# Queries and keys as seven block products per pair of panels, with the sums of the input formed in the gating stage

## Chip, cores and metric

One core of a Trainium2 chip runs the kernel. The metric is device time in microseconds (us) of one execution; less is better.

## What is computed

One step of a hybrid decoder layer for 512 prompt tokens and 64 sample tokens, 576 in all, with a model width of 1024. Cut to what matters here:

```
h = rmsnorm(x); z = h @ w_in                  # w_in: 1024 wide in, split into q, k, v, u, s, m and gates
q, k, v = zq, zk, zv                          # 1024 columns each: differential attention
o_sg = gelu(zu) * mix(rmsnorm(gelu(zs)))      # chunked spatial gating
merged = g0 * (o_da @ wb0) + g1 * (o_sg @ wb1) + g2 * (o_mx @ wb2)
x = x + merged @ w_out
a, b = split(rmsnorm(x) @ w_up); x = x + (silu(a) * b) @ w_down
```

The keys, the values and the normalised rows of s are outputs as well.

## The kernel before

Activations are kept transposed, 8 tiles of 128 features by 576 tokens. Every product is taken in three matmuls, of numbers split into a high and a low part in the fp32r type: hi times hi, lo times hi, hi times lo. Weights come in panels of 128 output columns (512 KB each) from one stream in HBM, `w_stream`, in the order of `STAGES`: mk and mv (memory keys and values), s, q, k, v, u, da_gate, and so on to w_out, the pairs of up, and down. A **plain panel** (`panel`, L1895) is 8 tiles x 3 terms x 2 halves of 288 tokens, 48 matmuls into a bank pair `acc[u]`. For each panel SP loads `w_raw[u]`, ScalarE copies it to `w_hi[u]` (`split_hi`, L696), VectorE forms `w_lo[u]` (`split_lo`, L1183), and ScalarE evacuates the result.

Each engine's program is written out by hand, and semaphores tie them together; nothing is scheduled by a planner. In the stage s the result goes through a gelu and is turned by TensorE in the next panel's shadow (`turning`, `turn_tile`), and VectorE copies it to `s_nat` (`nat_copy`). While q runs, ScalarE squares `s_nat`, GpSimd forms the factors (`g_rs`) and VectorE normalises (`nat_norm`, L1324). Each panel of k is followed by one mixing product of the gating (`mix`, L2053), and the panels of v are turned like those of s.

Only the stage up is done in **pairs**: 22 units of two panels, one of a, one of b. A unit splits its 2 x 2 blocks (weight halves by token halves) into seven products of 4 tiles x 3 terms, 84 matmuls of 128x288 (`product`, L2349). VectorE forms four weight sums per unit (`pair_sums`) and seven low parts (`lo_of`, L1585), ScalarE seven high parts (`hi_of`, L1061) and three copies of partial results (`product_copy`), and VectorE adds the partial results up (`up_unit`). The sums of the input (`xs_raw`, `xs_hi`, `xs_lo`) are formed tile by tile behind w_out's residual additions (L1595 to L1620). Products 0 to 3 of a unit have their split weights in the panel buffers `w_hi` and `w_lo`, products 4 to 6 in buffers of their own, `w_hi_b` and `w_lo_b`. The first unit's four weight sums are GpSimd's (L1873), and they begin once w_out's seventh panel is done. The norm's statistics of the new x (`norm_stats(2)`) run after product 1 of the first unit, and their broadcast after product 3.

Of the kernel before, what the change touches and what calls it, by code (L numbers as in the profile page):

```python
# [28 lines left out]
P = 128  # L29
# [28 lines left out]
STAGES = (("mk", 8), ("mv", 8), ("s", 8), ("q", 8), ("k", 8), ("v", 8), ("u", 8), ("da_gate", 8),  # L58
# [8 lines left out]
PAIRS = (("up", FT),)  # L67
# [5 lines left out]
STREAM_AT = {"up": FIRST["down"], "down": FIRST["down"] + 2 * FT}  # L73
# [4 lines left out]
BANK_OF = ("x", "z", "x", "z", "x", "w", "x")  # L78
BANK_START = (True, True, False, False, False, True, False)
# [24 lines left out]
def decoder_layer(nc, xT, memT, w_stream, page_table, cache_k, cache_v, mem_k, mem_v, consts,  # L104
# [3 lines left out]
    with ctx:  # L108
# [66 lines left out]
        nat_square, = at(merged_at, ("nat_square", [P, QT + 1, D]))  # L175
        sg = Region(x_at)
        norm_b = sg.take("norm_b", [P, D])
        sgb_b = sg.take("sgb_b", [P, GROUPS, P])
        sg_w = sg.take("sg_w", [P, GROUPS, P])
        sg_ws = Region(diag_at).take("sg_ws", [NS, GROUPS, NS])  # L180
# [82 lines left out]
        def pair_bank(j, s):  # L263

            return {"x": acc[0][:, s, 0:HT], "z": acc[1][:, 0, 0:HT], "w": acc[1][:, 1, 0:HT]}[BANK_OF[j]]

        def pair_raw(s, n, k):

            return (w_raw, w_raw_b)[s][:, n, k * KW:(k + 1) * KW]

        def pair_hi(j):
            return w_hi[:, j // 2, j % 2 * KW:(j % 2 + 1) * KW] if j < 4 else w_hi_b[:, j - 4, :]

        def pair_lo(j):
            return w_lo[:, j // 2, j % 2 * KW:(j % 2 + 1) * KW] if j < 4 else w_lo_b[:, j - 4, :]

        def pair_s(j, i=1):
            if isinstance(i, int) and i == 0:
                return w_sum[:, 1, :] if j == 1 else w_sum_b[:, {2: 1, 3: 2, 4: 0}[j], :]
            return w_sum[:, j, :] if j < 4 else w_sum_b[:, j - 4, :]  # L280
# [228 lines left out]
        def _(sp):  # L509
            def load_w(p, u, off=0):  # L510
# [4 lines left out]
            def stream(start, end, off=0):  # L515
# [4 lines left out]
            def load_pair(i, s, at):  # L520
# [3 lines left out]
                for n in range(2):  # L524
                    sp.dma_start((w_raw, w_raw_b)[s][:, n, :],
# [26 lines left out]
            for c in range(2):  # L552
                sp.dma_start(m_x[:, 4 * c:4 * c + 4, :], memT[4 * c * P:(4 * c + 4) * P, :]
                             .rearrange("(k p) n -> p k n", p=P)).then_inc(mem_loaded[c], 16)
                load_w(c, c)
# [5 lines left out]
            stream(2, FIRST["s"] + 4)  # L561
# [3 lines left out]
            stream(FIRST["s"] + 4, FIRST["s"] + 6)  # L565
            sp.wait_ge(line_stored, 16)
            for c in range(2):
# [5 lines left out]
            stream(FIRST["s"] + 6, FIRST["q"] + 2)  # L573
# [1939 lines left out]
```

## Time and profile before

| | us |
|---|---|
| median of 3 runs | 1344.37 (1343.51 to 1346.86) |
| the profiled execution | 1343.05 |
| its span | 1341.3 |
| TensorE busy in it | 1315.5 (98%) |
| VectorE, ScalarE, GpSimd busy | 667.9, 524.5, 89.9 |

The mean granted clock of TensorE is 0.992 of full speed. How to read it: TensorE is busy nearly throughout, so its timeline gives the stages' borders, and its few idle stretches lie at such borders. What TensorE waits for there is read from the timelines of VectorE, ScalarE and GpSimd in the same microseconds. Busy times of those three are averages over stages with different limits.

### The profile page before, as it was taken

The numbers are of one execution on the slowest core, as the hardware profiler recorded it, in microseconds if no ns is written. First come the engines' busy times: TensorE is split into PE (matmuls) and PEld (weight loads), VectorE is DVE, ScalarE is ACT, GpSimd is POOL, SyncE is SP. The second block draws the span as 40 slices with busy tenths as digits, with TensorE's granted clock in tenths as the row PEclk, the third lists the DMA queues.
The fourth block names the chain that finished last, engine by engine and source line by source line (L and its number), as shares of the span: only waits on it lengthen the run. The fifth ranks groups of instructions, "written<-read, shape, count | busy, mean of one in ns | idle before, by whom it ended". The sixth has DMA issues, their size and how long they took to land.

```text
span 1341.3 us, 25811 instructions
## 1 busy us (share of the span) xinstructions
PE 1315.5 (98%) x10082; PEld 1245.4 (93%) x10082; DVE 667.9 (50%) x1167; ACT 524.5 (39%) x1010; POOL 89.9 (7%) x129
## 2 busy tenths in 40 slices
PE   8899999999999999999999999998999999999997
PEld 8889999999888888888988889998999999999997
DVE  6643232223566532222344323567888888863333
ACT  5432321223477632222422343245555555552220
POOL 3620000000001010000000000001000000000001
PEclk9999999999999999999999999998999999999998
DMA  6544222524222197776589111432222222222221
GB/s 240 165 154 163 81 87 76 197 102 150 71 75 71 53 304 226 260 247 207 195 321 342 61 48 48 148 106 72 93 94 94 94 94 94 94 79 90 84 94 71
DMA packets 82087, 179.10 MB, mean 134 GB/s; under 512 B 5869, under 2 KB 40941, under 8 KB 80982
## 3 DMA queue, kind: packets, MB, share of 16 engines
q1 hardware_dynamic: 77750, 158.31, 34.7%
q10 hardware_dynamic: 2496, 12.58, 2.6%
q0 software_dynamic: 1760, 7.08, 1.5%
q8 instruction: 57, 0.93, 0.3%
q14 instruction: 24, 0.20, 0.0%
HBM read 166.13 MB, written 14.18 MB: 134 GB/s over the span
## 4 chain that ended last, share of the span: by engine, by line
PE 62%; issue 31%; DVE 2%; POOL 2%; ACT 1%; DMA 1%; POOLq 0%; SPq 0%; DVEq 0%; ACTq 0%
PE acc L1895 49%; PE ps L2107 2%; PE ps L2088 2%; PE ps L2164 1%; PE ps L2141 1%; PE ps L2272 1%; POOL ssum L1765 1%; PE ps L2288 1%; PE ps L2098 1%; PE ps L2239 1%; PE ps L1922 1%; PE ps L2053 1%; PE ps L2221 1%; DVE w_lo L1183 0%; DMA m_x<-memT 0%
## 5 line engine op out<-in xcount | busy, mean ns | idle before, releaser
L1183 DVE TENSOR_TENSOR w_lo<-w_raw,w_hi 128x1024 fp32r<-128x1024 f32 x144 | 178.0, 1236 | 369.7 <-ACT w_hi L696 368.8
L1895 PE MATMUL acc<-h_hi,w_hi 128*128 128x288 f32 x1152 | 263.2, 310 | 2.5 <-POOL h_lo L1745 2.4
L1895 PE MATMUL acc<-h_lo,w_hi 128*128 128x288 f32 x1152 | 247.5, 296 | 0.0
L1895 PE MATMUL acc<-h_hi,w_lo 128*128 128x288 f32 x1152 | 247.3, 296 | 0.0
L696 ACT ACTIVATE w_hi<-w_raw 128x1024 fp32r<-128x1024 f32 x144 | 152.0, 1056 | 156.4 <-PE acc L2376 74.6
L1895 PEld LDWEIGHTS acc<-h_hi,w_hi 128*128 128x128 f32 x1152 | 183.2, 189 | 13.8 <-issue 9.1
L1895 PEld LDWEIGHTS acc<-h_hi,w_lo 128*128 128x128 f32 x1152 | 184.7, 188 | 0.0
L1895 PEld LDWEIGHTS acc<-h_lo,w_hi 128*128 128x128 f32 x1152 | 184.7, 188 | 0.0
L2349 PE MATMUL acc<-xs_hi,w_hi 128*128 128x288 f32 x352 | 105.2, 299 | 3.5 <-DVE x_sb L1595 3.5
L2349 PE MATMUL acc<-xs_lo,w_hi 128*128 128x288 f32 x352 | 105.5, 300 | 0.0
L2349 PE MATMUL acc<-xs_hi,w_lo 128*128 128x288 f32 x352 | 105.4, 299 | 0.0
L2349 PE MATMUL acc<-xs_hi,w_hi_b 128*128 128x288 f32 x264 | 77.5, 294 | 0.9 <-issue 0.9
L2349 PE MATMUL acc<-xs_hi,w_lo_b 128*128 128x288 f32 x264 | 78.0, 296 | 0.0
L2349 PE MATMUL acc<-xs_lo,w_hi_b 128*128 128x288 f32 x264 | 77.8, 295 | 0.0
L2376 PE MATMUL acc<-g_lo,w_hi 128*128 128x288 f32 x352 | 75.7, 296 | 0.0
L2349 PEld LDWEIGHTS acc<-xs_hi,w_hi 128*128 128x128 f32 x352 | 67.3, 191 | 3.8 <-issue 3.8
L1895 PE MATMUL acc<-m_hi,w_hi 128*128 128x256 f32 (+1 forms) x256 | 65.4, 296 | 4.9 <-DVE w_lo L1183 4.3
L2349 PEld LDWEIGHTS acc<-xs_lo,w_hi 128*128 128x128 f32 x352 | 67.4, 191 | 0.0
L2349 PEld LDWEIGHTS acc<-xs_hi,w_lo 128*128 128x128 f32 x352 | 67.2, 191 | 0.0
L2376 PE MATMUL acc<-g_hi_main,w_hi 128*128 128x288 f32 x304 | 65.4, 296 | 0.0
L2376 PE MATMUL acc<-g_hi_main,w_lo 128*128 128x288 f32 x304 | 65.4, 296 | 0.0
L1895 PE MATMUL acc<-m_lo,w_hi 128*128 128x256 f32 (+1 forms) x256 | 64.0, 291 | 0.0
(330 smaller groups left out, 2410.6 us busy)
## 6 DMA issues: line engine op xcount, KB each, us to landing
w_raw<-w_stream SPq DMA_DIRECT2D x166, 512.0 KB, 3.5
v_pg<-cache_v SPq DMA_DIRECT2D x32, 512.0 KB, 5.5
w_raw_b<-w_stream SPq DMA_DIRECT2D x22, 512.0 KB, 4.2
k_even<-cache_k SPq DMA_DIRECT2D x16, 512.0 KB, 6.6
k_odd<-cache_k SPq DMA_DIRECT2D x16, 512.0 KB, 6.7
km_pg<-mem_k ACTq DMA_DIRECT2D x6, 1024.0 KB, 7.2
vm_pg<-mem_v ACTq DMA_DIRECT2D x6, 1024.0 KB, 7.3
x_sb<-xT SPq DMA_DIRECT2D x8, 576.0 KB, 6.0
```

The costliest lines, as they stand in the source:

```text
L696: nc.scalar.activation(w_hi[:, u, :], w_raw[:, u, :], ACT.Copy).then_inc(w_hi_done, 1)
L1183: nc.vector.tensor_tensor(w_lo[:, u, :], w_raw[:, u, :], w_hi[:, u, :].bitcast(F32), ALU.subtract)\
L1765: nc.gpsimd.tensor_tensor(ssum[:, :], sq_slot[0] if k == 1 else ssum[:, :], sq_slot[k % 2], ALU.add)\
L1895: last = nc.tensor.matmul(acc[a][:, c, 0:n], w[:, u, k * P:(k + 1) * P], x[:, k0 + k, c * n:(c + 1) * n], start=start and k == 0 and t == ...
L1922: last = nc.tensor.transpose(bank(4 + u)[:, j * P:(j + 1) * P], turn[:, u, j * P:(j + 1) * P], ident)
L2053: nc.tensor.matmul(bank(4 + u)[:, j * P:(j + 1) * P], s_nat[:, j, n * P:(n + 1) * P], sg_w[:, n, :], start=True, stop=True)
L2088: last = nc.tensor.matmul(bank(4 + c)[:, 0:w], qT[rows, h, i * P:(i + 1) * P], kT[rows, h, 0:w], start=True, stop=True)
L2098: last = nc.tensor.transpose(bank(6)[:, j * P:(j + 1) * P], a_p[:, m, j * P:(j + 1) * P], ident)
L2107: last = nc.tensor.matmul(bank(7)[:, i * DV:(i + 1) * DV], aT_p[:, m, j * P:(j + 1) * P], v_nat[:, j, h * DV:(h + 1) * DV], start=j == 0, ...
L2141: last = nc.tensor.matmul(bank(4 + c)[rows, 0:HK], q_blk[:, h, :], k_slot[e][:, h, c * HK:(c + 1) * HK], start=lane == 0, stop=lane == 1)
L2349: last = nc.tensor.matmul(pair_bank(j, s), w[:, k * P:(k + 1) * P], x[:, k, X_KIND[j], :], start=BANK_START[j] and k == 0 and t == 0, stop ...
L2376: last = nc.tensor.matmul(acc[a][:, c, 0:HT], w[:, u, k * P:(k + 1) * P], x[:, c * HT:(c + 1) * HT], start=start and k == 0 and t == 0, st ...
```

## The change

Queries and keys leave the list of plain stages and become 8 more pair units, ahead of the 22 of up (`PAIRS = (("qk", KT), ("up", FT))`, `QK = 8`). Units 0 to 3 give q, units 4 to 7 give k; from unit 4 on (`SWAP`) the two bank pairs change places. The sums of the input that these units need (`ht_raw`, four per tile pair) are formed by GpSimd during the stage s, split by ScalarE and VectorE, and kept in `x_sb`'s place. The sums of unit 0's weights are GpSimd's too. The mixing products of the gating move from the panels of k to those of v, and behind each panel of v there now stand a turn and a mix.

In every pair unit, of up too, products 0 to 2 now have the separate buffers (`w_hi_q`, `w_lo_q` for qk, `w_hi_b`, `w_lo_b` for up), and products 3 to 6 the panel buffers. At up's first unit the loads, sums and splits of products 0 to 2 are issued one tile earlier, product 0 waits for one bank pair instead of both, and GpSimd forms two of the four sums ahead of w_out's seventh panel. The unit that is last in up now has its raw weights in the panel buffers `w_raw`, and the splits of down's first two panels are put behind its products 4 and 6.

In the diff, the first loop over `QK` is ScalarE's, the second VectorE's; the loop over `KH` is GpSimd's and runs during the stage s; the last two pieces are ScalarE's in up's last unit.

```diff
-STAGES = (("mk", 8), ("mv", 8), ("s", 8), ("q", 8), ("k", 8), ("v", 8), ("u", 8), ("da_gate", 8),
+STAGES = (("mk", 8), ("mv", 8), ("s", 8), ("v", 8), ("u", 8), ("da_gate", 8),
...
-PAIRS = (("up", FT),)
+PAIRS = (("qk", KT), ("up", FT))
...
+        def pair_at(j, i, main, early, late):
+            if j < 3:
+                return (early if early_unit(i) else late)[:, j, :]
+            return main[:, (j - 3) // 2, (j - 3) % 2 * KW:((j - 3) % 2 + 1) * KW]
...
+            load_pair(0, 1, STREAM_AT["qk"])
...
+            sp.wait_ge(w_lo_done, FIRST["v"])
+            load_pair(1, 0, STREAM_AT["qk"])
+            sp.wait_ge(early_stored, 32)
             sp.dma_start(norm_b[:, :], ...).then_inc(sg_loaded, 16)
...
+            load_pair(2, 1, STREAM_AT["qk"])
             sp.wait_ge(g_zero, 1)
             for b in range(NB):
                 sp.dma_start(sg_ws[b * TS:(b + 1) * TS, ...
...
+            for i in range(3, QK):
+                load_pair(i, 1 - i % 2, STREAM_AT["qk"])
+            sp.wait_ge(pair_lo_done, NJ * QK)
+            stream(FIRST["v"], FIRST["v"] + 4)
...
+            for i in range(QK):
+                s, t, last = 1 - i % 2, i % 2, i == QK - 1
+                for c in range(3):
+                    product_copy(c, i, s, -(DK ** -0.5) if i < SWAP else 1.0)
+                    if not last:
+                        hi_of(c, i + 1, t)
+                if last:
+                    for u in range(2):
+                        act.wait_ge(pair_mm, NJ * i + 2 * u + 5)
+                        split_hi(FIRST["v"] + u, u)
...
+            for i in range(QK):
...
+                if i == 3:
+                    dve.wait_ge(g_rs, 1)
+                    dve.wait_ge(sg_loaded, 48)
+                dve.wait_ge(pair_mm, NJ * i + 4)
+                dve.wait_ge(pair_copied, 3 * i + 3)
+                nc.vector.scalar_tensor_tensor(dst[:, a, HT:T], pair_bank(3, i, s), scale, square[:, 0:HT],
+                                               ALU.mult, ALU.add).then_inc(pair_out, 1)
...
+            for k in range(KH):
+                nc.gpsimd.tensor_tensor(x1, h_hi[:, k, :].bitcast(F32), h_lo[:, k, :].bitcast(F32), ALU.add)
+                nc.gpsimd.tensor_tensor(x2, h_hi[:, KH + k, :].bitcast(F32), h_lo[:, KH + k, :].bitcast(F32), ALU.add)
+                nc.gpsimd.tensor_tensor(t1, x1[:, HT:T], x1[:, 0:HT], ALU.subtract).then_inc(x_diff, 1)
+                nc.gpsimd.tensor_tensor(t3, x2[:, HT:T], x1[:, HT:T], ALU.subtract).then_inc(x_diff, 1)
+                nc.gpsimd.tensor_tensor(t2, t3, x1[:, 0:HT], ALU.add).then_inc(x_diff, 1)
+                nc.gpsimd.tensor_tensor(t4, x2[:, 0:HT], t2, ALU.subtract).then_inc(x_diff, 1)
...
+            first_sums(0, FIRST["v"])
...
-            all_evacuated(pe, "down")
             for j in range(NJ):
-                product(j, 0, 0, first=True)
+                if j < 2:
+                    pe.wait_ge(acc_free[j], FIRST["down"] // 2)
+                product(j, QK, 1, first=True)
                 if j == 1:
                     norm_stats(2, T)
...
                 else:
-                    for u in range(2):
-                        act.wait_ge(pair_mm, NJ * (FT - 1) + 2 * u + 2)
-                        split_hi(FIRST["down"] + u, u)
+                    act.wait_ge(pair_mm, NJ * i + 5)
+                    split_hi(FIRST["down"], 0)
...
+                else:
+                    act.wait_ge(pair_mm, NJ * i + 7)
+                    split_hi(FIRST["down"] + 1, 1)
```

What the diff does not show at a glance is where VectorE's instructions stand at the two borders of up. The first place is VectorE at the end of w_out, before the change, from the squares' sum of tile 5 to that of tile 7 and the low parts behind it:

```order
L1218 TENSOR_TENSOR ssum<-ssum,gate 128x576 [waits summed,squared]
L1595 TENSOR_TENSOR x_sb<-acc,x_sb 128x576 [waits x_loaded1,mm_done]
...
L1585 TENSOR_TENSOR w_lo<-w_raw,w_hi 128x512 [waits pair_hi_done,mm_done]
L1585 TENSOR_TENSOR w_lo<-w_sum,w_hi 128x512 [waits pair_hi_done,pair_sum]
L1595 TENSOR_TENSOR x_sb<-acc,x_sb 128x576 [waits x_loaded3,mm_done]
...
L1218 TENSOR_TENSOR ssum<-ssum,gate 128x576 [waits summed,squared]
L1585 TENSOR_TENSOR w_lo<-w_sum_b,w_hi 128x512 [waits pair_hi_done,pair_sum,mm_done]
L1585 TENSOR_TENSOR w_lo<-w_sum_b,w_hi 128x512 [waits pair_hi_done]
L1585 TENSOR_TENSOR w_lo_b<-w_sum_b,w_hi_b 128x512 [waits pair_hi_done]
L1585 TENSOR_TENSOR w_lo_b<-w_raw,w_hi_b 128x512 [waits pair_hi_done,pair_lo_done] x2
```

And after the change, the same stretch (the residual addition is L1696 there, a low part L1397, the squares' sum L1277):

```order
L1277 TENSOR_TENSOR ssum<-ssum,gate 128x576 [waits summed,squared]
L1397 TENSOR_TENSOR w_lo_b<-w_raw_b,w_hi_b 128x512 [waits pair_hi_done]
L1397 TENSOR_TENSOR w_lo_b<-w_sum_b,w_hi_b 128x512 [waits pair_hi_done,pair_sum]
L1696 TENSOR_TENSOR x_sb<-acc,x_sb 128x576 [waits x_loaded1,mm_done]
...
L1397 TENSOR_TENSOR w_lo_b<-w_sum_b,w_hi_b 128x512 [waits pair_hi_done,pair_sum]
L1397 TENSOR_TENSOR w_lo<-w_sum,w_hi 128x512 [waits pair_hi_done] x2
L1696 TENSOR_TENSOR x_sb<-acc,x_sb 128x576 [waits x_loaded3,mm_done]
...
L1277 TENSOR_TENSOR ssum<-ssum,gate 128x576 [waits summed,squared]
L1397 TENSOR_TENSOR w_lo<-w_raw_b,w_hi 128x512 [waits pair_hi_done] x2
```

Five low parts instead of two now stand ahead of the last squares' sum, on which the statistics wait, and two instead of five behind it. The second place is VectorE in the last unit of up, after the change:

```order
L1751 TENSOR_TENSOR scaled<-cp,acc 128x288 [waits pair_mm]
L1242 TENSOR_TENSOR w_lo<-w_raw,w_hi 128x1024 [waits w_hi_done]
L1758 TENSOR_TENSOR scaled<-cp,acc 128x288 [waits pair_mm]
L1762 TENSOR_TENSOR scaled<-scaled,rms_b 128x576 [waits pair_out]
L1768 TENSOR_TENSOR g_sb<-gate,scaled 128x288 [waits ffn_silu]
L1770 TENSOR_TENSOR g_sb<-gate,acc 128x288 [waits pair_mm]
L1242 TENSOR_TENSOR w_lo<-w_raw,w_hi 128x1024 [waits w_hi_done]
L1778 TENSOR_TENSOR g_lo<-g_sb,g_hi_main 128x576 [waits ffn_hi] x10
```

Before, both splits of down's first panels (128x1024) stood two partial results higher, behind those of products 3 and 4; now they stand behind those of products 4 and 6, the second one ahead of the low parts of g.

## Rows read from the trace of the kernel before

**Rows 1.** The page's head and part 1: busy time, share, instructions of each engine.
```profile
span 1341.3 us, 25811 instructions
PE 1315.5 (98%) x10082; PEld 1245.4 (93%) x10082; DVE 667.9 (50%) x1167; ACT 524.5 (39%) x1010; POOL 89.9 (7%) x129
```
**Rows 2.** Timeline of TensorE, q's panel 1 and k's first mix (start, duration, engine, line).
```profile
137.25 0.52 PE L1895 MATMUL acc<-h_hi,w_hi 128*128 128x288 f32 x2
...
188.54 1.05 PE L2053 MATMUL ps<-sg_w,s_nat 128*128 128x128 f32 x8
```
**Rows 3.** Timeline of TensorE: starts of up's units 1 and 21, and of down.
```profile
946.91 0.30 PE L2349 MATMUL acc<-xs_hi,w_hi 128*128 128x288 f32 x1
...
1170.11 0.30 PE L2349 MATMUL acc<-xs_hi,w_hi 128*128 128x288 f32 x1
...
1181.32 0.43 PE L2376 MATMUL acc<-g_hi_late,w_hi 128*128 128x288 f32 x2
```
**Rows 4.** Busy time by stretch, up: PE, PEld, DVE, ACT, POOL, clock, DMA share, GB/s.
```profile
942.00:1186.00 244.00, 243.95 (x1836) 243.93 (x1837) 207.83 (x370) 135.33 (x246) 0.00 (x0) 1.00 0.25 91
```
**Rows 5.** Timeline of VectorE: up's unit 20, and the normalising in q.
```profile
165.91 2.47 DVE L1324 SCALAR_TENSOR_TENSOR s_nat<-s_nat,small,norm_b 128x1024 f32<-128x1024 f32 x2
...
1167.12 0.45 DVE L1659 TENSOR_TENSOR scaled<-cp,acc 128x288 f32<-128x288 f32 x1
...
1168.09 0.68 DVE L1585 TENSOR_TENSOR w_lo<-w_sum,w_hi 128x512 fp32r<-128x512 f32 x1
```
**Rows 6.** Timeline of GpSimd at the start of s, and in q.
```profile
79.16 1.41 POOL L1745 TENSOR_TENSOR h_lo<-square,h_hi 128x576 fp32r<-128x576 f32 x1
82.88 0.73 POOL L1782 DMA_DIRECT2D mv_out<-vm_new  x1 [1.84 <-ACT vm_new L751]
...
159.73 1.20 POOL L1793 TENSOR_TENSOR small<-small 128x5 f32<-128x5 f32 x1
```
**Rows 7.** Timeline of VectorE ahead of s and in s.
```profile
68.29 1.98 DVE L1262 SCALAR_TENSOR_TENSOR scaled<-x_sb,par,rms_b 128x576 f32<-128x576 f32 x1
...
76.93 0.81 DVE L1262 SCALAR_TENSOR_TENSOR square<-x_sb,par,rms_b 128x576 f32<-128x576 f32 x1
...
109.87 0.69 DVE L1306 COPY s_nat<-ps 128x512 f32 x1 [4.71 <-PE ps L1924]
```
**Rows 8.** Timeline of TensorE at the border of w_out and up.
```profile
929.60 0.58 PE L2349 MATMUL acc<-xs_hi,w_hi 128*128 128x288 f32 x1 [3.55 <-DVE x_sb L1595]
...
935.47 1.17 PE L1946 MATMUL ps<-cst,ssum 128*128 128x1 f32 x10
...
942.05 0.37 PE L2349 MATMUL acc<-xs_hi,w_hi_b 128*128 128x288 f32 x1 [0.91 <-issue]
```
**Rows 9.** Timeline of VectorE at the same border.
```profile
921.11 0.75 DVE L1595 TENSOR_TENSOR x_sb<-acc,x_sb 128x576 f32<-128x576 f32 x1
...
925.43 1.53 DVE L1603 TENSOR_TENSOR xs_lo<-xs_raw,xs_hi 128x288 fp32r<-128x288 f32 x1
...
928.75 0.74 DVE L1595 TENSOR_TENSOR x_sb<-acc,x_sb 128x576 f32<-128x576 f32 x1
...
933.58 0.75 DVE L1218 TENSOR_TENSOR ssum<-ssum,gate 128x576 f32<-128x576 f32 x1
```
**Rows 10.** TensorE's busy time by stretch at the same border: stretch, busy, clock, DMA.
```profile
926.00:929.60 3.60, 0.05 (x1) 0.86 0.00 0
929.60:933.00 3.40, 3.40 (x14) 0.50 0.00 0
```
**Rows 11.** Timeline of VectorE in up's last unit.
```profile
1179.93 0.45 DVE L1666 TENSOR_TENSOR scaled<-cp,acc 128x288 f32<-128x288 f32 x1
...
1182.66 6.77 DVE L1684 TENSOR_TENSOR g_lo<-g_sb,g_hi_main 128x576 fp32r<-128x576 f32 x10
```
**Rows 12.** The page's part 5: the splits of plain panels on VectorE and ScalarE.
```profile
L1183 DVE TENSOR_TENSOR w_lo<-w_raw,w_hi 128x1024 fp32r<-128x1024 f32 x144 | 178.0, 1236 | 369.7 <-ACT w_hi L696 368.8
...
L696 ACT ACTIVATE w_hi<-w_raw 128x1024 fp32r<-128x1024 f32 x144 | 152.0, 1056 | 156.4 <-PE acc L2376 74.6
```

More of the change, by code:

```diff
@@ L72 @@
     UNITS += _n
[L73 removed]
+QK = FIRST_PAIR["up"]
+STREAM_AT = {"qk": FIRST["v"], "up": FIRST["down"], "down": FIRST["down"] + 2 * QK + 2 * FT}
 NJ = 7
@@ new lines, in _, with nat_square_tile @@
+            for n in range(KT):
+                p, u = FIRST["s"] + n, n % 2
+                wait(act, turned, KT + n - 1)
+                evacuate(p, u, halves(turn[:, u, :]), ACT.Gelu_apprx_tanh)
+                if p + 2 < FIRST["v"]:
+                    split_hi(p + 2, u)
+                if 2 <= n < 2 + KH:
+                    ht_split(n - 2)
+                for j in ((0, 1, 2), (3, 4), (5, 6))[n - 5] if n >= 5 else ():
+                    hi_of(j, 0, 1)
+            def nat_square_tile(j):
+                rows = P if j < QT else NS
+                out = nat_square[:, j, :] if j < QT else nat_square_s[0:NS, :]
+                return nc.scalar.activation(out, s_nat[0:rows, j, :], ACT.Square, accum_out=col(G_SS + j, rows))
@@ L1310, in nat_copy, with ht_low @@
                 last.then_inc(nat_done, 1)
[L1312 to L1320 removed]
+            def ht_low(k):
+                dve.wait_ge(x_hi, k + 1)
+                nc.vector.tensor_tensor(ht_lo[:, k], ht_raw[:, k], ht_hi[:, k].bitcast(F32), ALU.subtract).then_inc(x_lo, 1)
@@ new lines, in product @@
+            def product(j, i, s, first=False):
+                pe.wait_ge(pair_lo_done, NJ * i + j + 1)
+                swap = early_unit(i) and i == SWAP
+                if not first:
+                    if j == 0:
+                        wait(pe, pair_out, 4 * (i - 1) + (3 if swap else 0))
+                    elif j == 1:
+                        wait(pe, pair_out, 4 * (i - 1) + (4 if swap else 1))
+                    elif j == 5:
+                        wait(pe, pair_out, 4 * (i - 1) + 3)
+                if j in (2, 3, 4):
+                    pe.wait_ge(pair_copied, 3 * i + j - 1)
+                elif j == 6:
+                    pe.wait_ge(pair_out, 4 * i + 2)
+                for k in range(KH):
+                    if first:
+                        pe.wait_ge(x_lo, XH + 4 * k + X_READY[j])
+                    elif early_unit(i) and i == 0 and j == 1:
+                        pe.wait_ge(x_lo, k + 1)
+                    x_hi_k, x_lo_k = pair_x(j, i, k)
+                    for t, (w, x) in enumerate(((pair_hi(j, i), x_hi_k), (pair_hi(j, i), x_lo_k), (pair_lo(j, i), x_hi_k))):
+                        last = nc.tensor.matmul(pair_bank(j, i, s), w[:, k * P:(k + 1) * P], x,
+                                                start=BANK_START[j] and k == 0 and t == 0, stop=k == KH - 1 and t == 2,
+                                                skip_group_check=not BANK_START[j])
+                last.then_inc(pair_mm, 1)
@@ L2045, in mix @@
+            pe.wait_ge(acc_free[0], FIRST["v"] // 2)
+            for i in range(QK):
+                for j in range(NJ):
+                    if i == 0 and j == 1:
+                        pe.wait_ge(acc_free[1], FIRST["v"] // 2)
+                    product(j, i, 1 - i % 2)
+                    if i == 0 and j == 2:
+                        turn_tile("s", KT - 1, 1, KT)
             def mix(n, u):
```

467 lines of the change are left out of this document (251 added, 216 removed).

## The prediction

> **What bounds the kernel now.** I read the page's first part, then the timeline of TensorE at the borders of the stages, then the other engines there. TensorE is busy 98% of the span [rows 1], so a matmul that goes is time, if what the change puts in its place keeps ahead of TensorE. In q the matmuls run without a gap: from panel 1's start at 137.25 to the first mix behind k's panel 0 at 188.54 are eight panels, 51.29 us, 6.41 us each [rows 2]. In up's pairs it is the same: from unit 1 at 946.91 to down at 1181.32 are 21 units, 234.41 us, 11.16 us each [rows 3], at full clock and with TensorE busy 243.95 of 244 us [rows 4]. So up shows what the changed stage would look like: seven products a unit, VectorE busy 207.83 of 244 us and ScalarE 135.33 [rows 4], neither in TensorE's way. The one border where TensorE stands still for long is that of w_out and up: 3.55 us idle, a low clock behind it, then 0.91 us [rows 8, 10].
>
> **Queries and keys.** Removed are 16 plain panels, 16 x 6.41 = 102.6 us; added are 8 units, 8 x 11.16 = 89.3 us. In matmuls: 768 of 128x288 go, 672 of the same size come. **-13.3 us**, all on the path. The eight mixes move from k to v with their cost, the turns stay.
>
> What must hide for it to be true:
>
> *VectorE per unit.* Per unit of up it is busy 207.83/244 x 11.16 = 9.5 us. A unit of qk has the same eleven 128x512 operations (0.68 each) and four partial results (0.45) [rows 5], and lacks up's multiplication by the norm and one product with the gate. Units 3 to 7 have one normalising of `s_nat` more, 2.47/2 = 1.24 us [rows 5], behind the unit's last low part. So some 9.5 us again, 1.6 us under TensorE's 11.16. Cost nothing; if a unit were paced by VectorE, each 0.68 us too much would cost 8 x 0.68 = 5.4 us.
>
> *GpSimd in s.* It is free at 82.88 + 0.73 = 83.6, and an addition of 128x576 with nothing beside it took 1.41 us [rows 6]. It gets 8 of these and 16 of 128x288, for which there is no row: between half of it (0.70) and all of it (1.41). That makes 22.6 to 33.8 us, so the input's sums are done between 106 and 117. I take the low end, for width governs VectorE's pair of 0.45 and 0.81 in the same way [rows 5, 7]. Two weight sums follow (1.41 each at most), then two more when s's seventh panel is done. Product 1 of unit 0, the first to read these sums, comes at about 132, so 11 us are in hand at the high end. Where GpSimd and VectorE both work, both are slow: VectorE's 0.81 became 1.98 [rows 7]. But in s VectorE idles 4.71 us ahead of each copy [rows 7], which holds two such delays.
>
> *The new waits.* VectorE now waits for the gating's factors and its loaded weights in unit 3, ahead of product 3's partial result, and behind that wait stand all of unit 4's sums and low parts. The squares end some 10 us into unit 2 (at about 163), the power takes 1.20 [rows 6], so the factors are there at 165, and VectorE comes by at about 169. SP's three gating loads now stand behind unit 1's load, at about 120, where they were before; the eight small ones behind unit 2's load, at about 133. Nothing.
>
> *From qk into v.* v's first panel can be split once product 4 of unit 7 has read the panel buffer: 5 x 1.6 = 8.0 us into the unit, plus 1.06 for ScalarE, plus 1.24 for VectorE [rows 12] is 10.3; the partial result of product 5 follows at 10.8, product 6 ends at 11.16. Nothing, with 0.4 us in hand; bounds 0 to +2.
>
> **The border of w_out and up.** Today VectorE is late here: it adds the residual of tile 6 at 921.11 and that of tile 7 at 928.75, and the squares' sum follows at 933.58 [rows 9]. TensorE waits for the tile-7 addition, runs products 0 and 1 at half speed, and starts the statistics at 935.47 [rows 8]. After the change product 0 needs only tile 6, and starts as w_out ends. But the statistics still wait for the last squares' sum, and ahead of it VectorE now has five low parts instead of two: 3 x 0.60 = +1.8 us. Two of GpSimd's four weight sums have gone from this stretch, where they stretched a 0.45 us operation to 1.53 [rows 5, 9]; I give back 1.2. So the statistics start within 0.6 us of where they do now: the hole in TensorE is cut in two, not filled. Behind the sum there are two low parts instead of five, so the broadcast and product 4 can come up to 1.2 us sooner. Against it stands the clock: it fell to 0.86 in the mean over the idle stretch and was 0.50 in the next, that is 1.2 GHz [rows 10], and products 0 and 1 took 5.87 us for 24 x 0.133 = 3.19. If it falls in one of the two new holes, products 2 and 3 pay that 2.7 us, part of which product 4's wait hides. **0 us**, bounds -1.2 and +2.
>
> The Trainium skill, "TensorE: Matmul & The Clock Gate", section "HAM oscillation", says that idle gaps between bursts of matmuls bring the clock back to half rate. By that, two holes with one short product between would lower it here as well, and the term would be +1 to +2 instead of 0; rows 10 agree for the one hole of today, and no row shows two in a row.
>
> The Trainium skill, "SBUF — State Buffer", section "Who interferes with whom", says that a VectorE operation with two inputs in SBUF and a GpSimd operation that reads SBUF shut each other out. It speaks against giving GpSimd 28 more additions in s; rows 7 agree with it, and by the idle time above the sum stays as it is.
>
> **From up into down.** This gets worse. Today the low part of g's tile 3 is done at 1182.66 + 0.68 = 1183.3 [rows 11], and down's first panel, begun at 1181.32 [rows 3], comes to that tile after 18 matmuls, at 1183.7: 0.4 us in hand. After the change the first split pushes product 5's partial result back by some 0.5 us (it began at 1179.93 [rows 11]; the split ends at 1180.4), and with it the silu; the second split then stands behind product 6, 1.06 us on ScalarE ahead of the high part of tile 3 and 1.24 us on VectorE ahead of its low part [rows 12]. Tile 3 is done near 1183.3 + 0.5 + 1.24 + 0.2 = 1185.3 instead of 1183.3. **+1.6 us**; bounds +0.8 (the second split alone, less the 0.4) and +2.5.
>
> **Sum.** -13.3 + 0 + 1.6 = -11.7 us. The profiled execution took 1343.05 us, and would take 1331.35; the median of the runs shown is 1.3 us above it, so 1332.7 us. From no change a measurement of this kernel can tell about 0.3%, 4.0 us.
>
> **Rivals.**
>
> *GpSimd comes too late (slower).* If its 24 additions and the two sums took over 1.75 us each in the mean, unit 0 would start late: 83.6 + 26 x 1.75 = 129, and ScalarE and VectorE, which hold s's evacuations behind these waits, would stop TensorE. At twice the 1.41, it is 83.6 + 26 x 2.82 = 157, and unit 0 begins near 160 instead of 130: 1332.7 + 30 = 1363 us. It decides the sign from 2.2 us each on. For it: VectorE's work in s is of the kind that slows it. Against: only 8 of 24 are full width, and 1.41 is the full width's price. Slower 0.04; between 1.75 and 2.2 each, no change, 0.05.
>
> *VectorE paces the units.* The chain sum, high part, low part, partial result runs over two engines, and one 0.68 us too much per unit gives 1332.7 + 5.4 = 1338.1. Against it: up runs the same chain without a stall. 0.08.
>
> *The clock stays high through the broken border.* Then product 4 comes 1.2 us sooner, and if the splits of down cost only their 0.8: -13.3 - 1.2 + 0.8 = -13.7, 1330.7 us. 0.15, inside my range.
>
> **How the numbers follow.** The forecast with all its bounds gets 0.80 (the high clock among it), VectorE's pacing 0.08, better than every bound 0.03: faster 0.91. Low end: 1330.7, less the 0.9 us by which the runs shown lie under their median, less a little for a border that I call nothing: 1329.3. High end: -13.3 + 2 + 2 + 2.5 = -6.8, so 1337.6, and 0.2 for VectorE's case: 1337.8.
>
> **What would show it.** Right: 672 matmuls of the pair kind between s and v, 89 us for them, no idle time of TensorE there; the wait of 3.55 us replaced by two shorter ones ahead of the statistics; a wait of 1 to 2 us for the low part of g in down's first panel, which today has none. Wrong: units of qk longer than 11.3 us, idle time ahead of unit 0 put down to GpSimd, or up's product 4 more than 2 us from its present distance of 16.4 us behind w_out's last matmul (925.6).

## The result and the profile after

The changed kernel took a median of **1336.88 us** over 8 runs (1334.64 to 1340.3), the kernel before 1344.36 us over 8 runs taken beside it (1343.51 to 1346.86): ratio 0.994, 95% interval [0.9928, 0.9953], 7.5 us faster. In a second set of runs on one chip it was 1336.79 against 1345.63 us, ratio 0.9938 [0.9925, 0.9951], 8.8 us faster. Forecast were 1332.7 us and 11.7 us less. The sign and the range hold, the median near the range's high end of 1337.8; some 3 to 4 us of the gain are missing, and the question is where.

The head of the page of the changed kernel answers to [rows 1]:

```profile
span 1335.9 us, 25775 instructions
PE 1307.6 (98%) x9986; PEld 1237.1 (93%) x9986; DVE 726.6 (54%) x1271; ACT 546.5 (41%) x1062; POOL 127.2 (10%) x157
```

TensorE has 96 matmuls less, as the change promises. VectorE gained 59 us of work and GpSimd 37, nearly all in s, q and k.

The timeline of TensorE in the changed kernel at the borders of that part (start, duration, engine, line) answers to [rows 2, 3]: the turn of s's panel 6, the starts of the units 1 and 7 of queries and keys, the first panel of v, the turn of v's last panel, then the starts of up's unit 1 and unit 21.

```profile
132.80 0.60 PE L2039 MATMUL ps<-cst,scaled 128*128 128x128 f32 x4
...
145.04 0.29 PE L2187 MATMUL acc<-h_hi,w_hi_q 128*128 128x288 f32 x1
...
211.93 0.29 PE L2187 MATMUL acc<-h_hi,w_hi_q 128*128 128x288 f32 x1
...
223.08 0.30 PE L2012 MATMUL acc<-h_hi,w_hi 128*128 128x288 f32 x1
...
296.10 0.60 PE L2039 MATMUL ps<-cst,scaled 128*128 128x128 f32 x4
...
939.07 0.29 PE L2187 MATMUL acc<-xs_hi,w_hi_b 128*128 128x288 f32 x1
...
1162.94 0.29 PE L2187 MATMUL acc<-xs_hi,w_hi_b 128*128 128x288 f32 x1
```

A unit of queries and keys takes (223.08 - 145.04) / 7 = 11.15 us, without idle time of TensorE anywhere between 133 and 300 us. A unit of up takes (1162.94 - 939.07) / 20 = 11.19 us, where it took 11.16 [rows 3].

What TensorE waited for in the changed kernel (the view of waits: total, times, longest) shows where the new kernel stands still:

```profile
PE acc L2012 <- DVE w_lo L1242: 4.0, 4, 1.8
PE ps L2063 <- DVE ssum L1277: 2.8, 1, 2.8
PE acc L2187 <- DVE x_sb L1696: 2.5, 1, 2.5
...
PE acc L2514 <- DVE g_lo L1778: 1.5, 1, 1.5
...
PE acc L2187 <- DVE xs_lo L1704: 0.7, 1, 0.7
```

The one wait of 3.55 us [rows 8] has become three, of 0.7, 2.5 and 2.8 us, and down has one of 1.5 that it did not have.

The whole span can be cut at events that both kernels have. Each kernel was profiled twice (the second profiles are the first and the fifth experiment below). "w_out's end" is the time at which its next matmul would have started.

| from, to | before | before, 2nd | changed | changed, 2nd |
|---|---|---|---|---|
| start to the turn of s's panel 6 | 129.84 | 132.22 | 132.80 | 131.70 |
| to the turn of v's last panel | 176.52 | 176.52 | 163.30 | 163.30 |
| to w_out's end | 619.53 | 619.49 | 619.49 | 619.52 |
| to up's product 4 | 16.16 | 17.03 | 18.58 | 16.99 |
| to down | 239.27 | 239.27 | 240.04 | 240.04 |
| to down's end | 140.80 | 140.80 | 142.61 | 142.61 |
| to the end | 19.18 | 18.17 | 19.08 | 19.14 |
| span | 1341.3 | 1343.5 | 1335.9 | 1333.3 |

Four rows repeat to 0.04 us: -13.22, 0, +0.77, +1.81. Three do not (the front, the border of w_out and up, the end), and between the first two profiles alone they hid 5.3 us of the gain: 2.96 + 2.42 - 0.10.

### The profile page after: what moved, and what is told of

Its sections match the earlier page's. It is cut to its first block, busy times and chain, and to the rows that moved or that the text cites. A ratio compares the mean times of both kernels' runs of the same rounds, so it can differ in the third digit from the quotient of the medians.

```text
span 1335.9 us, 25775 instructions
## 1 busy us (share of the span) xinstructions
PE 1307.6 (98%) x9986; PEld 1237.1 (93%) x9986; DVE 726.6 (54%) x1271; ACT 546.5 (41%) x1062; POOL 127.2 (10%) x157
## 4 chain that ended last, share of the span: by engine, by line
PE 62%; issue 31%; DVE 3%; POOL 2%; ACT 1%; DMA 1%; POOLq 0%; SPq 0%; ACTq 0%; DVEq 0%
PE acc L2012 42%; PE acc L2187 7%; PE ps L2267 2%; PE ps L2248 2%; PE ps L2324 1%; PE ps L2301 1%; PE ps L2432 1%; POOL ssum L1859 1%; PE ps L2448 1%; PE ps L2258 1%; PE ps L2399 1%; PE ps L2039 1%; PE ps L2209 1%; PE ps L2381 1%; DVE w_lo L1242 0%
## 5 line engine op out<-in xcount | busy, mean ns | idle before, releaser
L1242 DVE TENSOR_TENSOR w_lo<-w_raw,w_hi 128x1024 fp32r<-128x1024 f32 x128 | 160.9, 1257 | 298.5 <-ACT w_hi L733 298.0
L2012 PE MATMUL acc<-h_hi,w_hi 128*128 128x288 f32 x896 | 208.0, 314 | 2.5 <-POOL h_lo L1839 2.4
L733 ACT ACTIVATE w_hi<-w_raw 128x1024 fp32r<-128x1024 f32 x128 | 135.2, 1056 | 168.2 <-PE acc L2514 74.9
L2012 PE MATMUL acc<-h_lo,w_hi 128*128 128x288 f32 x896 | 193.0, 297 | 0.0
L2012 PE MATMUL acc<-h_hi,w_lo 128*128 128x288 f32 x896 | 192.8, 297 | 0.0
L2012 PEld LDWEIGHTS acc<-h_hi,w_hi 128*128 128x128 f32 x896 | 142.8, 190 | 13.8 <-issue 9.1
L2012 PEld LDWEIGHTS acc<-h_hi,w_lo 128*128 128x128 f32 x896 | 144.3, 189 | 0.0
L2012 PEld LDWEIGHTS acc<-h_lo,w_hi 128*128 128x128 f32 x896 | 144.2, 189 | 0.0
L844 ACT ACTIVATE w_hi<-w_sum 128x512 fp32r<-128x512 f32 x60 | 37.8, 632 | 67.6 <-DVE w_sum L1389 40.6
```

What stands on the lines that cost most here:

```text
L733: nc.scalar.activation(w_hi[:, u, :], w_raw[:, u, :], ACT.Copy).then_inc(w_hi_done, 1)
L844: nc.scalar.activation(pair_hi(j, i), pair_part(j, i, s), ACT.Copy).then_inc(pair_hi_done, 1)
L1242: nc.vector.tensor_tensor(w_lo[:, u, :], w_raw[:, u, :], w_hi[:, u, :].bitcast(F32), ALU.subtract)\
L2012: last = nc.tensor.matmul(acc[a][:, c, 0:n], w[:, u, k * P:(k + 1) * P], x[:, k0 + k, c * n:(c + 1) * n], start=start and k == 0 and t == ...
```

## The experiments

The times are medians of 4 to 6 runs (one run where it is said), and the changed kernel ran again beside the first three edits only. The 95% intervals of the ratios reach some 2 us to either side, and those of the last two kernels below are the only ones that lie clear of the changed kernel's [0.9925, 0.9951]. A difference of 1.6 to 2.9 us from the changed kernel is therefore no proof by itself: what such an edit does is read from its stage in the trace, which is one execution.

**The changed kernel once more**, with no edit, to see what of this belongs to the change.

> The changed kernel as it is, profiled once more. Against the kernel before, the first profile gives by stage: 3.0 us later at the turn of s's panel 6 (132.80 instead of 129.84), -13.2 from there to v's last turn, 2.6 us more in the border of w_out and up, 0.8 more in up (21 units of 11.195 instead of 11.16), 1.8 more in down. Theory A: the 3.0 us in front are no part of the change, but the clock level of that execution at 20 to 25 us and at 82 to 86 us; then this profile has the turn of s's panel 6 at another time, anywhere from 129.8 to 133. Theory B: the change moves something there; then it stands at 132.8 within 0.3 again. The border (18.6 us from w_out's last matmul to product 4) and down's wait of 1.5 us for g's low part come again under both. Time under both: 1335 to 1338 us.

Measured: 1336.79 us; the turn at 131.70, not at 132.80; the border 16.99, not 18.58; up, down and the wait of 1.54 us as before. So theory A for the front. The expectation that the border comes again was wrong. It is the clock. TensorE's busy time by stretch in the border, first profile of the changed kernel (stretch, its length, busy time and instructions of PE, PEld, DVE, ACT, POOL, then clock, DMA share, GB/s):

```profile
917.70:920.80 3.10, 0.63 (x3) 0.40 (x3) 3.06 (x5) 0.68 (x3) 0.00 (x0) 1.00 0.00 0
920.80:922.90 2.10, 2.08 (x12) 1.73 (x12) 1.23 (x3) 1.53 (x3) 0.00 (x0) 0.85 0.00 0
922.90:925.60 2.70, 0.00 (x0) 0.00 (x0) 2.68 (x7) 2.65 (x6) 0.00 (x0) 0.50 0.00 0
925.60:932.50 6.90, 6.84 (x29) 6.84 (x30) 4.28 (x13) 1.96 (x6) 1.19 (x1) 0.50 0.41 152
```

And in the second, the same four stretches, 1.1 us earlier:

```profile
916.60:919.70 3.10, 0.66 (x3) 0.43 (x3) 3.09 (x5) 0.70 (x2) 0.00 (x0) 0.99 0.00 0
919.70:921.80 2.10, 2.05 (x8) 2.06 (x9) 1.20 (x3) 1.51 (x3) 0.00 (x0) 0.50 0.00 0
921.80:924.50 2.70, 1.19 (x5) 0.84 (x4) 2.68 (x7) 2.65 (x6) 0.00 (x0) 0.77 0.00 0
924.50:930.40 5.90, 5.82 (x34) 5.82 (x35) 4.30 (x13) 1.99 (x6) 1.18 (x1) 0.71 0.47 176
```

The statistics and product 4 in the first, then in the second:

```profile
925.66 2.29 PE L2063 MATMUL ps<-cst,ssum 128*128 128x1 f32 x10 [2.76 <-DVE ssum L1277]
...
934.17 0.38 PE L2187 MATMUL acc<-xs_hi,w_hi 128*128 128x288 f32 x1
```

```profile
924.58 1.28 PE L2063 MATMUL ps<-cst,ssum 128*128 128x1 f32 x10 [1.59 <-DVE ssum L1277]
...
931.51 0.38 PE L2187 MATMUL acc<-xs_hi,w_hi 128*128 128x288 f32 x1
```

In the first, the clock falls inside product 1 and stays at half through the third hole, the statistics and products 2 and 3. In the second it is already low when product 1 starts, comes back in the third hole, and falls again behind it for a shorter time. The same program, with the statistics 10.07 us behind w_out's end in both; 1.6 us between the two. Three kernels further down leave this border as it is, and their traces give the same two lengths: 17.0 us (down's second split moved; s's first panel filled) and 18.6 (more work for VectorE in queries and keys).

**TensorE held back until both bank pairs are free**, so that products 0 and 1 run without a gap.

```diff
-                if j < 2:
-                    pe.wait_ge(acc_free[j], FIRST["down"] // 2)
+                if j == 0:
+                    for u in range(2):
+                        pe.wait_ge(acc_free[u], FIRST["down"] // 2)
```

> TensorE waits for the last residual ahead of product 0 instead of ahead of product 1, so that products 0 and 1 run without a gap, as they did in the kernel before. Theory clock (two holes with one product between keep the clock at 1.2 GHz through the statistics and products 2 and 3): products 0 and 1 go slower, about 5.9 us, but the statistics take 1.2 instead of 2.3 us and products 2 and 3 take 3.3 instead of 5.4; product 4 starts 16.0 to 17.2 us behind w_out's last matmul instead of 18.6: 1.4 to 2.6 us faster, although TensorE starts later. Rival (VectorE's three low parts ahead of the last squares' sum set the border): nothing is gained and product 0's early start is lost: 0 to 1.6 us slower.

Measured: 1335.13 us, ratio 0.9924 [0.9911, 0.9937]: 1.7 us below the changed kernel run beside it. Timeline of TensorE: first product, statistics, product 4:

```profile
921.44 0.45 PE L2187 MATMUL acc<-xs_hi,w_hi_b 128*128 128x288 f32 x1 [5.12 <-issue]
...
926.23 1.28 PE L2063 MATMUL ps<-cst,ssum 128*128 128x1 f32 x10
...
932.35 0.37 PE L2187 MATMUL acc<-xs_hi,w_hi 128*128 128x288 f32 x1 [0.52 <-issue]
```

TensorE starts 5.3 us later and is earlier at product 4 (16.19 us behind w_out's end): in this trace the head start that the change gives product 0 is worth less than nothing, by 0.8 us against the shorter of the two lengths above and 2.4 against the longer.

**The two long holes filled** with 16 and 20 matmuls that nobody reads.

```diff
+                if j == 1:
+                    fill(16)
                 if j < 2:
                     pe.wait_ge(acc_free[j], FIRST["down"] // 2)
                 product(j, QK, 1, first=True)
                 if j == 1:
+                    fill(20)
                     norm_stats(2, T)
```

> Adds 36 matmuls of 128x288 to a bank that nobody reads: 16 ahead of product 1, 20 behind it, each set shorter than the idle time there (2.48 and 2.76 us). Theory clock: it stays at 2.4 GHz, the statistics take 1.2 instead of 2.3 us, products 2 and 3 take 3.3 instead of 5.4, product 4 comes 15.3 to 15.7 us behind w_out's last matmul instead of 18.6: 2.9 to 3.3 us faster. Rival (VectorE's work and not the clock sets the border): product 4 keeps its 18.6 us within 0.5, no change of the time.

Measured: 1333.87 us, ratio 0.9912 [0.9897, 0.9926], 2.9 us below the changed kernel; no stretch of the border is below full clock. Product 4 comes at 16.19 us, not at 15.3 to 15.7: with the clock high it waits 0.51 us itself, for the copy of product 2 behind the norm's chain (statistics on TensorE, a column of 128x5 numbers on VectorE, a power on GpSimd, diagonals on VectorE, the broadcast on TensorE). The clock theory holds. So 16.2 us is the changed border's length by its queues, and the clock adds 0.8 and 2.4 us in the two profiles of the changed kernel.

In the kernel before the clock adds nothing in either profile, although products 0 and 1 run at half speed in both: the norm's chain goes on when VectorE has done the five low parts behind the last squares' sum. It reads the statistics' column (`small<-ps`) 11.37 us behind w_out's end in the first profile, and in the changed kernel with its holes filled, where only two low parts stand there but the sum comes later, at 11.39:

```profile
937.26 0.16 DVE L1190 TENSOR_SCALAR small<-ps 128x5 f32<-128x5 f32 x1
```

```profile
928.20 0.16 DVE L1249 TENSOR_SCALAR small<-ps 128x5 f32<-128x5 f32 x1 [0.17 <-PE ps L2063]
```

The 0.87 us by which the border is longer in the second profile of the kernel before are GpSimd's. Its four weight sums, which the trace shows waiting for a load of `w_raw`, began 3.67 us ahead of w_out's end and not 4.95, so that the last of them ran beside one operation more of VectorE, tile 6's squares' sum. The last weight sum and that operation in the first profile, then in the second:

```profile
925.27 1.38 POOL L1873 TENSOR_TENSOR w_sum_b<-w_raw 128x512 f32<-128x512 f32 x1
926.88 0.75 DVE L1218 TENSOR_TENSOR ssum<-ssum,square 128x576 f32<-128x576 f32 x1
```

```profile
928.85 1.36 POOL L1873 TENSOR_TENSOR w_sum_b<-w_raw 128x512 f32<-128x512 f32 x1
929.01 1.81 DVE L1218 TENSOR_TENSOR ssum<-ssum,square 128x576 f32<-128x576 f32 x1
```

Tile 7's squares' sum, the column (12.24 us) and product 4 are all later by this 0.86 to 0.87.

**Down's second split behind g's tile 7** on ScalarE and VectorE.

```diff
-                    act.wait_ge(pair_mm, NJ * i + 7)
-                    split_hi(FIRST["down"] + 1, 1)
...
                 g_hi_tile(k)
+                if k == 7:
+                    split_hi(FIRST["down"] + 1, 1)
...
                 g_lo_tile(k)
+                if k == 7:
+                    split_lo(FIRST["down"] + 1, 1)
```

> The split of down's second panel moves behind the high and low part of g's tile 7 on ScalarE and VectorE. Theory (the split in front of g's tile 3 costs its length, as the prediction has it): the wait of 1.54 us for g's low part in down's first panel shrinks to 0.2 to 0.5, and down's second panel starts with a wait of at most 0.3: 0.8 to 1.3 us faster. Rival (the last unit's chain of product 6, silu and gate sets tile 3, the split only fills its idle time): the wait stays at 1.3 to 1.5 us and the second panel waits besides: 0 to 1 us slower.

Measured: 1334.58 us, ratio 0.992 [0.9907, 0.9932], 2.2 us below the changed kernel, of which the trace gives 1.35 to down (141.26 instead of 142.61 us). The wait in the changed kernel:

```profile
1178.31 0.54 PE L2514 MATMUL acc<-g_hi_main,w_hi 128*128 128x288 f32 x2 [1.54 <-DVE g_lo L1778]
```

And with the split behind tile 7:

```profile
1174.87 0.54 PE L2513 MATMUL acc<-g_hi_main,w_hi 128*128 128x288 f32 x2 [0.19 <-DVE g_lo L1775]
```

**The kernel before once more**, with no edit.

> The kernel before, profiled a second time. In its first profile the clock fell once ahead of s (at 44 us) and not in s's first panel, and the turn of s's panel 6 was at 129.84; in five profiles of the changed kernel it stood at 131.7 to 133.35, with the clock low at 80 to 86 us in every one. Theory A (the clock there is a matter of the execution, not of the change): this profile shows a low clock at 78 to 86 us or a second one ahead of s too, and the turn at 131 to 133. Theory B (the change brings it): the turn is at 129.8 within 0.4 again, no low clock in s's first panel.

Measured: one run, 1345.28 us, and the turn at 132.22. Theory A: the front belongs to the execution. The stretch in which s's first panel lies (columns as above), in its first profile:

```profile
78.00:88.00 10.00, 8.44 (x61) 8.20 (x62) 1.22 (x1) 3.96 (x6) 3.77 (x4) 1.00 0.31 113
```

And in this one:

```profile
78.00:88.00 10.00, 8.19 (x50) 7.95 (x51) 1.46 (x3) 4.87 (x7) 3.96 (x5) 0.83 0.32 110
```

The first profile was a lucky one: clock 1.00 there, 0.83 in this one and in both of the changed kernel. How often shows in all the kernels of this document: of the 11 profiles without filling matmuls in s, 8 read 0.83 there and 3 read 1.00, one of the kernel before and two of edited kernels (low parts behind the sum; more work for VectorE).

**Low parts behind the last squares' sum.**

```diff
-                    if n < KT - 1:
+                    if n < KT - 2:
                         first_lows(QK, n - (KT - 3))
+            first_lows(QK, 1)
             first_lows(QK, 2)
```

> VectorE's three low parts (products 2, 3 and 4 of up's unit 0) move from ahead of the last residual to behind the last squares' sum. Theory: they cost the statistics their 3 x 0.60 = 1.8 us, so these start 8.3 us behind w_out's last matmul instead of 10.07, and product 1 1.8 us sooner; product 4 gains less, since the five low parts then stand between the sum and the diagonals: 15.9 to 16.5 us instead of 17.0 to 18.6, 0.5 to 2 us faster, by the clock that stays high in shorter holes. Rival (the residual of tile 7 waits for something else than these three operations): statistics at 10 us as before, no change.

Measured: 1334.82 us, ratio 0.9923 [0.991, 0.9937]. The statistics start 8.27 us behind w_out's end, where they started at 10.07: 1.80 us, the three low parts to the hundredth. Product 4 stands at 16.79, not at 15.9 to 16.5: the clock fell here too, the statistics took 2.27 us, and part of the gain went there.

**GpSimd's last two weight sums to VectorE**, behind the last squares' sum, with the low parts there too. ScalarE's high parts of products 3 and 4, which read these sums, move with them behind w_out's last panel (not shown below).

```diff
-                                    (3, a12, pair_s(2, i), ALU.subtract), (4, a11, a21, ALU.subtract)):
+                                    (3, a12, pair_s(2, i), ALU.subtract), (4, a11, a21, ALU.subtract))[:4 if i < QK else 2]:
...
+            pair_sums(3, QK, 1)
+            pair_sums(4, QK, 1)
+            first_lows(QK, 1)
             first_lows(QK, 2)
```

> GpSimd's last two weight sums of up's unit 0, which run beside VectorE's work for tile 5 and stretch it (0.45 to 1.56 and 0.75 to 1.85 us, 2.2 in all), go to VectorE behind the last squares' sum; the three low parts stand there too. Theory (the prediction gave back 1.2 us for two sums gone, but the two that are left still cost 2.2): the two operations take 0.45 and 0.75, the statistics start at 10.07 - 1.8 - 2.2 = 6.1 us behind w_out's last matmul, product 4 at 14.5 to 16 instead of 17.0 to 18.6: 1.5 to 3.5 us faster. Rival (the stretch is hidden by the wait for w_out's panels): statistics at 8.3 as with the low parts alone, product 4 at 16 to 17.

Measured: 1334.24 us, ratio 0.9926 [0.9913, 0.994]; the statistics at 6.05 us, product 4 at 15.50. VectorE in the changed kernel, with GpSimd's sums running from 909.49 to 912.50:

```profile
909.77 1.56 DVE L1721 TENSOR_TENSOR xs_lo<-scaled,xs_hi 128x288 fp32r<-128x288 f32 x1
911.26 1.85 DVE L1277 TENSOR_TENSOR ssum<-ssum,gate 128x576 f32<-128x576 f32 x1
```

And the same two operations without them:

```profile
908.70 0.45 DVE L1717 TENSOR_TENSOR xs_lo<-scaled,xs_hi 128x288 fp32r<-128x288 f32 x1
909.07 0.75 DVE L1273 TENSOR_TENSOR ssum<-ssum,gate 128x576 f32<-128x576 f32 x1
```

The two sums cost VectorE 1.11 + 1.10 us, and the statistics the same 2.2 (8.27 to 6.05).

**S's first panel filled** with 12 matmuls that nobody reads.

```diff
             def h_tile(k):
+                if k == 6:
+                    for _ in range(12):
+                        nc.tensor.matmul(bank(7)[:, 0:HT], h_hi[:, 0, 0:P], h_hi[:, 0, 0:HT], start=True, stop=True)
```

> Adds 12 matmuls of 128x288 to a bank that nobody reads in s's first panel, ahead of the wait of 1.75 us for the low part of input tile 6. Theory clock: the clock no longer falls at 80 to 86 us, s's first panel and the next lose no 1.7 us: 1 to 1.7 us faster, the turn of s's panel 0 at 17.2 us or less behind s's first matmul where the profiles have 17.0 to 18.4 (16.3 in the kernel before, where the clock stayed). Rival (GpSimd's additions or VectorE's stretched splits slow s's start, not the clock): the turns stay where they are, no change.

Measured: 1334.92 us, ratio 0.9924 [0.991, 0.9937], 1.9 us below the changed kernel's 1336.79. The clock is 1.00 from 78 to 88 us, the turn of s's panel 0 stands 16.32 us behind s's first matmul, and that of panel 6 at 129.84, as in the lucky profile. GpSimd's additions are all still there: they are not what slowed s's start. That the fill did it is not shown by this trace alone, since the clock also stayed at 1.00 in the two edited kernels without a fill named above, with that turn at 16.31 and 16.30 us; in the eight profiles at 0.83 it stands at 17.04 to 18.40. For the fill speaks that both kernels that have it read 1.00. Behind the turn of panel 0, panel 6's follows 41.7 us later in every profile of both kernels, so past its entry the change costs s nothing.

**More work for VectorE in queries and keys**: a second subtraction ahead of three low parts per unit, into a buffer that is free then.

```diff
                 dve.wait_ge(pair_hi_done, NJ * i + j + 1)
+                if early_unit(i) and i and j in (0, 5, 6):
...
+                    nc.vector.tensor_tensor(rms_b[:, 0:KW], pair_part(j, i, s),
+                                            pair_hi(j, i).bitcast(F32), ALU.subtract).then_inc(spare_done, 1)
```

> Units 0 to 6 of the queries and keys get three more operations of 128x512 on VectorE (0.60 us apart each, 1.8 per unit), written to a buffer that nobody reads then, ahead of the low parts of the next unit's products 0, 5 and 6. VectorE is busy 54.94 of 67 us there, 9.15 of 11.15 us a unit; with them 10.95. Theory (cover of 2.0 us a unit, as the prediction costed it at nothing): units stay at 11.15 us within 0.05, TensorE idles less than 1 us in all, no change of the time (within 1.5 us of the changed kernel). Rival (the chain sum, high part, low part, partial result paces the units as soon as VectorE is late in it): units of 11.4 to 12.5 us, waits of TensorE for low parts or partial results, 2 to 9 us slower.

Measured: 1338.42 us, ratio 0.9952 [0.9936, 0.9967], 1.6 us above the changed kernel. Units 1 and 2 stay at 11.15 us, unit 3 takes 12.24, units 4 to 6 take 11.42 each. Busy time by stretch of this kernel: units 1 and 2, unit 3, units 4 to 6 (columns as above):

```profile
142.50:164.80 22.30, 22.30 (x170) 22.30 (x169) 19.73 (x35) 14.14 (x27) 0.19 (x1) 1.00 0.27 96
164.80:177.00 12.20, 11.35 (x86) 11.15 (x85) 11.06 (x20) 6.53 (x14) 1.38 (x2) 1.00 0.25 87
177.00:211.30 34.30, 34.21 (x254) 33.59 (x253) 33.90 (x58) 15.80 (x30) 0.00 (x0) 1.00 0.18 62
```

Neither side was right throughout. Where VectorE has the normalising too, it is busy 33.90 of 34.30 us and paces the units; the mean of 9.15 us had averaged that away. In the changed kernel itself VectorE has 29.29 of 33.40 us there, a cover of 1.4 us a unit, and 16.35 of 22.30 in the units before, 3.0.

**The border in another order**, nothing added: the sums on VectorE, ScalarE's copies of products 0 to 2 ahead, and of the low parts behind the sum only those of products 2 and 3 ahead of the diagonals.

```diff
+            product_copy(0, QK, 1)
+            product_copy(1, QK, 1)
+            for j in (3, 4, 5, 6):
+                hi_of(j, QK, 1)
...
+            pair_sums(3, QK, 1)
+            first_lows(QK, 1)
+            norm_small(2, T)
+            pair_sums(4, QK, 1)
+            lo_of(3, QK, 1)
+            norm_diag(2, T)
+            lo_of(4, QK, 1)
             first_lows(QK, 2)
-            norm_stats(2, T)
```

> The border of w_out and up written in another order, and nothing added: GpSimd's last two weight sums go to VectorE behind the last squares' sum; VectorE then does the low part of product 2, the statistics' column, the low part of product 3, the diagonals, and only then the low parts of products 4, 5 and 6; ScalarE copies products 0 and 1 ahead of the high parts and product 2 ahead of the next unit's. Theory (VectorE's and ScalarE's queues set the border once the sums no longer collide, the clock takes what is left): statistics 6.1 us behind w_out's last matmul, product 4 at 11.5 us with the clock high and up to 13.5 with it low, where the changed kernel has 17.0 to 18.6: 3.5 to 6 us faster than the changed kernel, 1331 to 1333.5 us. Rival (another wait, such as the power on GpSimd or the copies' order, takes over): product 4 at 15 or later, as with the sums alone (15.5), 1334 us.

Measured: 1333.51 us, ratio 0.9904 [0.9889, 0.992]; product 4 at 14.50 us, between the two expectations: the statistics took 2.29 us and products 2 and 3 ran at half clock.

**The parts that won, together**: that border with 19 filling matmuls, down's late split, the fill in s.

> The border as in border_only with 19 matmuls into a bank that nobody reads ahead of the statistics, down's second split behind g's tile 7, and 12 such matmuls in s's first panel: the parts that single runs found faster. If the gains add: 1336.8 less 1.5 (s's entry) less 5 (border, product 4 at 11.5 to 12.5) less 1.4 (down) is 1328.9 us, 1327.5 to 1331. Rival (the fills only move the low clock to another place, and border and down overlap in nothing): the sum falls short by 2 us or more, 1331 to 1333.

Measured: **1329.67 us** (1329.43 to 1329.87, 4 runs), ratio to the kernel before 0.9883 [0.9868, 0.9898]; 7.1 us below the changed kernel's 1336.79 and 15.9 below the kernel before, 1345.56 beside it. Timeline of TensorE: product 0, statistics, product 4, and product 6 of the same unit:

```profile
914.51 0.30 PE L2205 MATMUL acc<-xs_hi,w_hi_b 128*128 128x288 f32 x1
...
920.56 1.28 PE L2074 MATMUL ps<-cst,ssum 128*128 128x1 f32 x10 [0.19 <-DVE ssum L1282]
...
926.19 0.38 PE L2205 MATMUL acc<-xs_hi,w_hi 128*128 128x288 f32 x1
...
931.27 0.37 PE L2205 MATMUL acc<-xs_hi,w_hi 128*128 128x288 f32 x1 [1.63 <-DVE w_lo_b L1402]
```

The time lies inside the expected range, and the clock is full in the whole border. Product 4 comes at 11.68 us, 5.3 to 6.9 sooner than in the changed kernel; 1.63 of it is given back at product 6, which needs the bank that VectorE empties with product 4's partial result (the view names the low part that had just ended; the partial result runs from 930.72 to 931.17). That one now stands behind the next unit's sums and low parts, and VectorE's queue is the late one. The runs lie within 0.5 us of each other, where those of the changed kernel spread over 4 to 6.

## Why the prediction was right, and where not

*Queries and keys, -13.3 us.* Right: -13.22 in both pairs of profiles, units of 11.15 us, no idle time.

*"Cost nothing", VectorE.* Right: 9.15 us a unit against the estimate of 9.5. That it has a limit at hand, 1.4 us further in units 4 to 6, the added load showed.

*GpSimd in s.* Right in the result, low in price: an addition of 128x288 took 0.80 us alone, not 0.70, and up to 1.85 beside VectorE's splits; the 24 were done at 117.6, just past the high end of what was said. Product 1 of unit 0 came 17 us later. The rival that it comes too late fell.

*The new waits, and from qk into v.* Right: the factors were there at 169.2, VectorE came to them at 174; v began without a wait.

*"The border: cut in two, not filled; 0 us."* This is the step that failed, by its size. Its queues come out at 0, 16.19 us with full clock against the 16.16 of the first profile, but in part by luck: two pieces of the working were mis-sized and cancel. "I give back 1.2", for two of GpSimd's sums gone, came to some 0.25: the two that stay cost 2.2 us, where the stretch in the kernel before cost 2.5 (1.33, 0.96 and 1.53 instead of 0.46, 0.46 and 0.45). So the last squares' sum was ready 10.0 us behind w_out's end instead of 8.4, 1.6 later. Against it, the three low parts that no longer stand behind the sum gave back nearly the same, not "up to 1.2": VectorE reads the statistics' column at 11.39 us where it read it at 11.37. The statistics themselves start at 10.07 instead of 9.58, within the 0.6 that was said, since the kernel before started them 1.1 us after the sum was ready, behind products 0 and 1 at half speed. What the term lacked is the clock, which the text put at 2.7 us "part of which product 4's wait hides" and then at nothing: it cost 0.8 to 2.4 us. The statement on what would be wrong, product 4 more than 2 us from its old distance, came true in the first profile and not in the second.

The prediction set beside this the Trainium skill, "TensorE: Matmul & The Clock Gate", section "HAM oscillation", which says that idle gaps between bursts of matmuls bring the clock back to half rate. From it the prediction made +1 to +2 us, an estimate; that sizes the clock's part better than my 0, and the filled holes agree: with them no stretch of the border is below full clock. The other rule that it named from the Trainium skill, "SBUF — State Buffer", section "Who interferes with whom", that VectorE with two inputs in SBUF and GpSimd reading SBUF shut each other out, was set against s only, where idle time hid it. In the border nothing hides it, and there the two sums cost the 2.2 us.

*From up into down, +1.6 us.* Right: the wait is 1.54, down 1.81 longer, and moving the second split takes 1.35 of it away.

*Not in the sum: up's units.* They take 0.035 us more each, 0.77 in all, in every profile of the changed kernel, spread over all seven products, with no idle time and the same number of TensorE's instructions per unit. The cause is open; only the buffers are other ones.

*The base.* The stages were read from an execution of 1343.05 us, and the forecast set against a median of 1344.37. The medians of the kernel before in the later sets, 1344.36 to 1345.63, show that the execution was a good one, and its front had a low clock at one place where most other profiles have two or three.

The account, then: of the 11.7 us, 0.8 went to up, 0.2 to down, and 1.0 to the border, by the means of the two profiles of the kernel before (16.6 us) and of the five with the changed border as it is (17.6), which leaves 9.7. Measured were 7.5 and 8.8 us; the 0.9 to 2.2 that are missing lie where executions of one and the same kernel differ, in the front and at the end. Whether the change moves their mean stays open: two profiles of the kernel before do not tell it.

The rival "VectorE paces the units" needs 1.4 us more per unit than the kernel has. "The clock stays high through the broken border" happened in none of the nine profiles without filling matmuls there. Made to happen, it gives 1333.87 us, and product 4 comes at 16.19 us, not 1.2 us sooner than before: that part of the rival was wrong too.

## What to carry to other kernels

Starting TensorE early on a short piece of work, with nothing behind it, can lose time: here the clock fell in or behind such holes and ran the products that came next at half, and a later start without a gap, or matmuls that nobody reads, brought product 4 forward by 0.8 to 2.4 us. Profile both kernels twice before a term of one or two microseconds is read from the difference of two traces; the rows that repeat to the hundredth are the ones to believe. A mean busy share of a stage hides its fullest unit, so the cover for added work is to be read unit by unit.

## Not expected of the hardware

- The same program has its clock low at other places from execution to execution: the stretch from 78 to 88 us read 1.00 and 0.83 in two profiles of the kernel before, and the border of the changed kernel took 17.0 us in three traces and 18.6 in two. The end reads 18.2 us or 19.1 in the same way. With the holes filled in s and in the border, four runs lay within 0.5 us.
- The ten statistics matmuls of one column took 1.17 to 1.28 us at full clock and 2.27 to 2.29 at half.
- A VectorE operation of 0.45 us took 1.56 beside GpSimd's 128x512 addition, and one of 0.75 took 1.85: the same 1.1 us, not a fixed factor. In the kernel before, others of 0.46 us took 0.96 and 1.33.
